# Feed-forward in-products by Strassen's scheme in a decoder trunk, with ScalarE copying products between PSUM banks

## The chip, the cores and the metric

One NeuronCore of a Trainium2 chip runs the whole program in one launch. The metric is the device time of that core in microseconds. All arithmetic is in 32-bit floats.

## The reference

One inference step of a two-layer decoder on 544 tokens: 512 of a prompt and 8 samples with 4 tokens each. Layer 0 mixes tokens with RWKV-7, layer 1 with sparse attention. Before and after each mixer stands a half-step feed-forward, so there are four of them, each with its own weights:

```python
def swiglu(x, w_in, w_out):
    gate, up = jnp.split(x @ w_in, 2, axis=-1)
    return (jax.nn.silu(gate) * up) @ w_out

h = h + 0.5 * swiglu(rms_norm(h, g[0]), ffn_w_in[l, 0], ffn_w_out[l, 0])
h = h + mixer(rms_norm(h, g[1]))
h = h + 0.5 * swiglu(rms_norm(h, g[2]), ffn_w_in[l, 1], ffn_w_out[l, 1])
```

The model width is 1024 (8 tiles of 128 features), the feed-forward width 2816 (22 tiles). So `x @ w_in` has 22 gate and 22 up tiles.

## The kernel before

Activations lie with features on the partitions and the 544 tokens along the row, in two halves of 272 (`HALF`), since a PSUM bank holds 512 floats. The residual is `hT`, 8 tiles of 544.

Every feed-forward product keeps its precision by splitting both operands in a high part in TensorE's reduced format (`fp32r`) and a low part (the rest). ScalarE copies a weight slot from `raw` to `wh` (the high part, L1133), VectorE subtracts it to get `wl` (L1484), and TensorE computes high x high + high x low + low x high. That is the helper `times` (L518): three matmuls for each weight tile and half. Each matmul has a weight load of its own.

The work of a feed-forward `f` is in stages that share two slots `s` (two buffers in `raw`, `wh` and `wl`, four PSUM banks each): `inA` with 12 of the 22 feature tiles, `outA`, `inB` with 10, `outB`. One slot of an in-stage is one feature tile: 8 input tiles for gate (banks 4s, 4s+1) and 8 for up (banks 4s+2, 4s+3), 96 matmuls. VectorE scales the gate by the reciprocal root `rr` (L1553), ScalarE takes silu (L1194), VectorE multiplies with the up part (L1556), ScalarE copies the high part to `hh` (L1196) and VectorE makes the low part `hl` (L1560). One slot of an out-stage is one of 8 output tiles: VectorE scales it (L1582) and adds it to `hT` (L1586). In the last out-stage ScalarE squares the new `hT` tile (L1177) and VectorE sums the squares in `acc` (L1522); from these come the norm's sum on TensorE (L509), the root on ScalarE (L1184) and the reciprocal on VectorE (L1526).

The operand of an in-stage is `xh` (ScalarE, L1163) and `xl` (VectorE, L1532), `hT` times the norm's gain; the root is applied afterwards through `rr`. In the second and fourth feed-forward the operand is made as the stage before (`wo` and `bo`) ends, and the norm comes in the first in-slot, between its gate and its up.

The order on each engine is the order in the program. `pipeline` on ScalarE and VectorE puts the split of the next slot before the finishing of this one. SP's queue brings the weights: `stream_split` waits for `w_split[s]`, then loads 1 MB for an in-slot. Semaphores named here: `landed[s]` (weights there), `w_hi[s]`, `w_split[s]`, `multiplied[s]` (TensorE is through), `taken[s]` (the banks are free), `gate_done`, `hid_hi`, `hid_done`. GpSimd issues other loads and has arithmetic only in the mixers (L2057, L2147).

## Time and profile before

| what | value |
|---|---|
| median of 3 runs | 2955.61 us (2951.46 to 2957.7) |
| the profiled execution: own time | 2960.64 us |
| its span | 2959.0 us |
| TensorE busy (matmul / weight load) | 2794.9 us (94%) / 2551.7 us (86%) |
| VectorE, ScalarE, GpSimd busy | 1185.8 us (40%), 806.5 us (27%), 282.6 us (10%) |
| matmuls | 25,177 |
| mean granted clock of TensorE | 0.942 |

The span is the time from the first instruction to the last one; the own time is what the same execution took as a whole. The busy share of matmuls is an upper bound, since they are pipelined. The granted clock is a share of 2.4 GHz; 0.5 is 1.2 GHz.

### The profile page before, as it was taken

How to read it: one execution, taken by the hardware profiler on the slowest of the kernel's cores; microseconds unless marked ns; L12 is line 12 of the kernel's file. 1: busy time of each engine (PE TensorE's matmuls, PEld its weight loads, DVE VectorE, ACT ScalarE, POOL GpSimd, SP SyncE). 2: the span in 40 equal slices, each digit the busy share in tenths (PEclk: the TensorE clock that was granted, in tenths of full speed). 3: DMA queues.
4: the chain of work that ended last, by engine and by line, in shares of the span. 5: the costliest groups of instructions: out<-in, count | busy, mean ns of one | idle time of the engine just before them, and what ended most of it. 6: DMA issues, size and time to landing. Idle time of an engine off the chain costs nothing. (4 is left out here: it accounts for less than half of the span.)

```text
span 2959.0 us, 56832 instructions
## 1 busy us (share of the span) xinstructions
PE 2794.9 (94%) x25177; PEld 2551.7 (86%) x25177; DVE 1185.8 (40%) x1738; ACT 806.5 (27%) x1261; POOL 282.6 (10%) x288
## 2 busy tenths in 40 slices
PE   7999969998999899999998989999998889999997
PEld 7999966776899746999997879999995568999997
DVE  4333355176333251433334123333444443433335
ACT  4212212132222100222221053212226762322221
POOL 1000000001111110000001200000007860000000
PEclk9999989999998557999998999999998997999998
DMA  6222210210000000322224622222222010222222
GB/s 233 82 89 86 77 64 15 71 58 30 4 3 4 33 29 26 131 82 80 95 69 120 162 100 85 85 100 85 71 74 65 23 44 29 88 90 79 99 69 75
DMA packets 36806, 214.84 MB, mean 73 GB/s; under 512 B 5232, under 2 KB 5360, under 8 KB 20880
## 3 DMA queue, kind: packets, MB, share of 16 engines
q1 hardware_dynamic: 27936, 174.34, 17.1%
q0 software_dynamic: 8720, 38.28, 4.4%
q8 instruction: 121, 1.98, 0.3%
q14 instruction: 29, 0.24, 0.0%
HBM read 202.49 MB, written 12.17 MB: 73 GB/s over the span
## 5 line engine op out<-in xcount | busy, mean ns | idle before, releaser
L518 PE MATMUL banks<-xh,wh 128*128 128x272 f32 x3072 | 638.7, 289 | 30.3 <-DVE wl L1484 18.0
L518 PE MATMUL banks<-xh,wl 128*128 128x272 f32 x3072 | 637.5, 289 | 0.0
L518 PE MATMUL banks<-xl,wh 128*128 128x272 f32 x3072 | 635.0, 288 | 0.0
L518 PEld LDWEIGHTS banks<-xh,wh 128*128 128x128 f32 x3072 | 485.5, 189 | 31.1 <-DVE wl L1484 23.4
L518 PEld LDWEIGHTS banks<-xl,wh 128*128 128x128 f32 x3072 | 484.7, 189 | 0.0
L518 PEld LDWEIGHTS banks<-xh,wl 128*128 128x128 f32 x3072 | 481.2, 189 | 0.0
L1484 DVE TENSOR_TENSOR wl<-raw,wh 128x2048 fp32r<-128x2048 f32 (+2 forms) x160 | 323.9, 2024 | 109.8 <-ACT wh L1133 109.7
L1133 ACT ACTIVATE wh<-raw 128x2048 fp32r<-128x2048 f32 (+2 forms) x160 | 270.7, 1692 | 260.5 <-PE banks L518 243.9
L518 PE MATMUL banks<-hh,wl 128*128 128x272 f32 x1408 | 291.4, 288 | 0.0
L518 PE MATMUL banks<-hh,wh 128*128 128x272 f32 x1408 | 291.0, 288 | 0.0
L518 PE MATMUL banks<-hl,wh 128*128 128x272 f32 x1408 | 290.2, 288 | 0.0
L1194 ACT ACTIVATE sg<-sg 128x544 f32<-128x544 f32 x88 | 58.1, 660 | 700.6 <-DVE sg L1553 700.6
L1553 DVE TENSOR_TENSOR sg<-banks,rr 128x544 f32<-128x544 f32 x88 | 63.8, 725 | 439.5 <-PE banks L518 439.5
L586 PE MATMUL banks<-arena,raw 128*128 128x272 f32 x896 | 209.9, 398 | 13.0 <-DVE arena L1540 10.4
L518 PEld LDWEIGHTS banks<-hh,wh 128*128 128x128 f32 x1408 | 221.4, 188 | 0.0
L518 PEld LDWEIGHTS banks<-hl,wh 128*128 128x128 f32 x1408 | 221.3, 189 | 0.0
L518 PEld LDWEIGHTS banks<-hh,wl 128*128 128x128 f32 x1408 | 219.8, 189 | 0.0
L586 PEld LDWEIGHTS banks<-arena,raw 128*128 128x128 f32 x896 | 172.6, 193 | 51.0 <-issue 14.9
L1582 DVE SCALAR_TENSOR_TENSOR sg<-banks,rr 128x544 f32<-128x544 f32 x64 | 46.4, 725 | 243.1 <-PE banks L518 243.1
L665 PE MATMUL banks<-arena,raw 128*128 128x272 f32 x512 | 120.4, 394 | 4.1 <-issue 4.1
L665 PEld LDWEIGHTS banks<-arena,raw 128*128 128x128 f32 x512 | 96.6, 190 | 27.3 <-issue 7.8
L2147 POOL TENSOR_SCALAR arena<-arena,stats 128x128 f32<-128x128 f32 (+3 forms) x108 | 116.0, 1087 | 40.6 <-DVE stats L1943 40.3
(301 smaller groups left out, 3030.6 us busy)
## 6 DMA issues: line engine op xcount, KB each, us to landing
raw<-in_w_in SPq DMA_DIRECT2D x88, 1024.0 KB, 4.8
raw<-in_w_out SPq DMA_DIRECT2D x32, 768.0 KB, 4.2
raw<-in_w_out SPq DMA_DIRECT2D x32, 640.0 KB, 3.9
raw<-in_w_rk SPq DMA_DIRECT2D x8, 1024.0 KB, 4.8
arena<-in_pages_c POOLq DMA_DIRECT2D x32, 256.0 KB, 7.6
raw<-in_w_kv SPq DMA_DIRECT2D x6, 1024.0 KB, 4.8
raw<-in_w_v SPq DMA_DIRECT2D x4, 1024.0 KB, 4.8
raw<-in_w_o SPq DMA_DIRECT2D x4, 1024.0 KB, 4.8
```

What stands on the lines that cost most here:

```text
L518: ins = mm(pst[:, bank + half, 0:HALF], wt[:, s, w], a[:, half * HALF:(half + 1) * HALF], start=first, stop=last)
L586: last = mm(pst[:, 4 * s + 2 * m + half, 0:HALF], w, src[:, ft, half * HALF:(half + 1) * HALF], start=(ft == 0), stop=(ft == DT - 1))
L665: last = mm(pst[:, 2 * w0 + half, 0:HALF], w, src[:, ft, half * HALF:(half + 1) * HALF], start=(ft == 0), stop=(ft == DT - 1))
L1133: act.activation(wh[:, s, 0:cols], raw[:, s, 0:cols], ACT.Copy).then_inc(w_hi[s], 1)
L1194: act.activation(sg[:, s, :], sg[:, s, :], ACT.Silu).then_inc(gate_done[s], 1)
L1484: dve.tensor_tensor(wl[:, s, 0:cols], raw[:, s, 0:cols], wh[:, s, 0:cols].bitcast(F32), ALU.subtract)\
L1553: dve.tensor_tensor(halves(sg[:, s, :]), bank2(4 * s), halves(rr[:]), ALU.mult)\
L1582: dve.scalar_tensor_tensor(out=halves(sg[:, s, :]), in0=bank2(4 * s), scalar=factor, in1=halves(rr[:]), op0=ALU.mult, op1=ALU.mult)\
L2147: ins = pool.tensor_scalar(s[:, c], s[:, c], stats[:, x, 4, 3 * p + n:3 * p + n + 1], None, ALU.mult)
```

## The change

The in-product of one feature tile, `[1024 inputs] x [gate and up] x [2 token halves]`, is taken as a 2 x 2 by 2 x 2 product of blocks: the inputs in even and odd tiles (4 each), the outputs in gate and up, the tokens in their two halves. Strassen's scheme in Winograd's form gives it by seven block products in place of eight, with sums of operand blocks ahead and sums of products behind. A block product is one token half with 4 weight tiles: 12 matmuls (`eighth`), so a slot has 84.

- Weights: of each slot VectorE makes four sums of 512 elements (`sums_w`), and the split to high and low goes by seven parts of 512 (`ring_h` on ScalarE, `ring_l` on VectorE), each as soon as TensorE has used the same part of the slot before.
- Operands: four sums in each of the four pairs of input tiles, by GpSimd (`operand_sums`); their high parts by ScalarE, their low parts by VectorE (`low_operands`). They are made once for each feed-forward, in its opening.
- Products: TensorE accumulates in bank x; ScalarE copies x to bank y, later x to w and x to z, and w to `sg`, and TensorE accumulates further products on these copies. VectorE adds the two results for up. All four banks are then the slot's gate and up. In the first two slots of a feed-forward 6 extra matmuls go to banks y and z.
- Stages: four in-stages (6, 6, 6 and 4 feature tiles) and four out-stages for each feed-forward. The first pair of slots of an out-stage is interleaved tile by tile. Out-stages A to C have 6 tiles a slot, D has 4.
- The reciprocal root (`inverse_root`) stands in VectorE's first in-slot between the second and third part; the root goes to `rr` and no longer to `sg`.
- Some of GpSimd's loads wait for the end of in-stage D (`part_split`).

The core of the diff. The block product:

```diff
+            def eighth(bank, quarter, f, b, js, start, stop):
+                for j in js:
+                    w = slice((4 * quarter + j) * P, (4 * quarter + j + 1) * P)
+                    xh_j, xl_j = xop_h[f][j][:, b, :], xop_l[f][j][:, b, :]
+                    for wt, x, first, last in ((ring_h, xh_j, start and j == 0, False), (ring_h, xl_j, False, False),
+                                               (ring_l, xh_j, False, stop and j == 3)):
+                        ins = mm(pst[:, bank, 0:HALF], wt[:, w], x, start=first, stop=last, skip_group_check=True)
+                return ins
```

TensorE, one in-slot (the first of a feed-forward has another order, as its operands come one by one):

```diff
+                pe.wait_ge(taken[s], i + k0)
+                part(0)
+                    eighth(x_bank, 0, f, 0, range(4), True, True).then_inc(eighth_done, 1)
+                    part(1)
+                    eighth(w_bank, 1, f, 5, range(4), True, True).then_inc(eighth_done, 1)
+                    part(2)
+                    snapped(1)
+                    eighth(x_bank, 2, f, 4, range(4), False, True).then_inc(eighth_done, 1)
+                    part(3)
+                    eighth(y_bank, 3, f, 1, range(4), False, True).then_inc(eighth_done, 1)
+                    part(4)
+                    snapped(3)
+                    eighth(x_bank, 4, f, 3, range(4), False, True).then_inc(eighth_done, 1)
+                pe.wait_ge(w_split[s], i + (ks + 1))
+                eighth(w_bank, 5, f, 6, range(4), False, True).then_inc(eighth_done, 1)
+                part(6)
+                snapped(4)
+                eighth(z_bank, 6, f, 2, range(4), False, True).then_inc(multiplied[s], 1)
```

ScalarE, slot `t`; `following(e)` is the high part `e` of slot `t + 1`:

```diff
+                    act.wait_ge(eighth_done, 6 * k + 1)
+                    act.activation(y, x, ACT.Copy).then_inc(snap, 1)
+                    following(0)
+                    act.wait_ge(eighth_done, 6 * k + 2)
+                    act.activation(sg[:, s, 0:HALF], w, ACT.Copy).then_inc(snap, 1)
+                    following(1)
+                    act.wait_ge(eighth_done, 6 * k + 3)
+                    act.activation(w, x, ACT.Copy).then_inc(snap, 1)
+                    if t == 0 and n is not None:
+                        norm(n, 4)
+                    if t:
+                        tail(t - 1)
+                    following(2)
+                    act.wait_ge(eighth_done, 6 * k + 4)
+                    following(3)
+                    act.wait_ge(eighth_done, 6 * k + 5)
+                    act.activation(z, x, ACT.Copy).then_inc(snap, 1)
+                    following(4)
+                    act.wait_ge(eighth_done, 6 * k + 6)
+                    following(5)
+                    act.wait_ge(multiplied[s], k0 + t // 2 + 1)
+                    following(6)
+                    act.wait_ge(taken[s], k0 + t // 2 + 1)
+                    act.activation(sg[:, s, :], sg[:, s, :], ACT.Silu).then_inc(gate_done[s], 1)
```

VectorE, slot `t`; `following(e)` is part `e` of slot `t + 1` (for `e` under 4 a weight sum first, then the low part):

```diff
+                    following(0)
+                    following(1)
+                    if t:
+                        tail(t - 1)
+                    if t == 0 and before:
+                        before()
+                    following(2)
+                    following(3)
+                    dve.wait_ge(snap, 4 * k + 4)
+                    dve.tensor_tensor(up[1], x, sg[:, s, 0:HALF], ALU.add).then_inc(up_done, 1)
+                    following(4)
+                    dve.wait_ge(eighth_done, 6 * k + 6)
+                    dve.tensor_tensor(up[0], w, sg[:, s, 0:HALF], ALU.add).then_inc(up_done, 1)
+                    following(5)
+                    dve.wait_ge(multiplied[s], k0 + t // 2 + 1)
+                    dve.wait_ge(up_done, 2 * k + 2)
+                    dve.tensor_tensor(halves(sg[:, s, :]), pst[:, 4 * s + 2:4 * s + 4, 0:HALF], halves(rr[:]), ALU.mult)                       .then_inc(taken[s], 1)
+                    following(6)
+                    dve.wait_ge(gate_done[s], h)
+                    dve.tensor_tensor(halves(sg[:, s, :]), halves(sg[:, s, :]), up_both, ALU.mult)                       .then_inc(hid_ready[s], 1)
```

TensorE, the first pair of slots of an out-stage:

```diff
+                for x in range(2):
+                    pe.wait_ge(hid_done[x], hidden + tiles // 2 - 1)
+                for s in range(2):
+                    take_split(s, k0, ks)
+                    for ft in range(tiles - 2):
+                        tile(s, ft)
+                pe.wait_ge(hid_done[0], hidden + tiles // 2)
+                for s in range(2):
+                    tile(s, tiles - 2)
+                pe.wait_ge(hid_done[1], hidden + tiles // 2)
+                for s in range(2):
+                    tile(s, tiles - 1).then_inc(multiplied[s], 1)
```

GpSimd, for each pair `j` of input tiles:

```diff
+                pool.wait_ge(xg_done, 8 * f + 2 * j + 1)
+                pool.tensor_tensor(t1, b12, b11, ALU.subtract).then_inc(t_step, 1)
+                pool.wait_ge(xg_done, 8 * f + 2 * j + 2)
+                pool.wait_ge(t_step, 8 * f + 2 * j + 1)
+                pool.tensor_tensor(t2, b22, t1, ALU.subtract).then_inc(t_step, 1)
+                pool.tensor_tensor(t3, b22, b12, ALU.subtract)
+                pool.wait_ge(t_step, 8 * f + 2 * j + 2)
+                pool.tensor_tensor(t4, b21, t2, ALU.subtract).then_inc(xt_done, 1)
```

## Rows read from the trace of the kernel before

**Rows 1.** The page: busy shares, and the granted clock in 40 slices.

```profile
PE 2794.9 (94%) x25177; PEld 2551.7 (86%) x25177; DVE 1185.8 (40%) x1738; ACT 806.5 (27%) x1261; POOL 282.6 (10%) x288
...
PEclk9999989999998557999998999999998997999998
```

**Rows 2.** Windows of the four feed-forwards: stretch, its length, busy us, clock, DMA.

```profile
18.00:432.00 414.00, 402.35 (x3176) 400.78 (x3176) 169.74 (x165) 104.00 (x103) 7.43 (x13) 0.99 0.30 100
...
sum 1620.00, PE 1602.11 PEld 1599.82 DVE 651.50 ACT 420.87 POOL 11.90; mean PE 400.53 PEld 399.96 DVE 162.87 ACT 105.22 POOL 2.98
```

**Rows 3.** Waits of TensorE: us in total, times, longest.

```profile
PE banks L518 <- DVE xl L1532: 7.1, 1, 7.1
```

**Rows 4.** Timeline of TensorE in an in-slot: start, us, instruction.

```profile
99.74 0.41 PE L518 MATMUL banks<-xh,wh 128*128 128x272 f32 x2
...
105.75 0.41 PE L518 MATMUL banks<-xh,wh 128*128 128x272 f32 x2
```

**Rows 5.** Timeline of VectorE: the scaling at a slot's end.

```profile
118.73 0.72 DVE L1553 TENSOR_TENSOR sg<-banks,rr 128x544 f32<-128x544 f32 x1 [4.93 <-PE banks L518]
```

**Rows 6.** Timeline of VectorE: operations back to back.

```profile
429.75 0.69 DVE L1635 TENSOR_TENSOR arena<-arena 128x511 f32<-128x511 f32 x1
430.36 0.15 DVE L1636 TENSOR_SCALAR arena<-arena 128x1 f32<-128x1 f32 x1
...
2492.71 5.17 DVE L2011 TENSOR_TENSOR xl<-arena,xh 128x544 fp32r<-128x544 f32 x8
```

**Rows 7.** Groups by line and shape on VectorE: count, busy us, mean ns.

```profile
L1484 DVE TENSOR_TENSOR wl<-raw,wh 128x2048 fp32r<-128x2048 f32 x96 | 220.0, 2292 | 94.9 <-ACT wh L1133 94.8
...
L1532 DVE SCALAR_TENSOR_TENSOR xl<-arena,const,xh 128x544 fp32r<-128x544 f32 x40 | 30.2, 781 | 15.9 <-ACT xh L1163 15.9
...
L1526 DVE RECIPROCAL rr<-sg 128x544 f32<-128x544 f32 x7 | 24.9, 3550 | 9.8 <-ACT sg L1184 9.8
...
L1926 DVE CUSTOM_DVE_ANT_0 arena<-banks,arena 128x256 f32<-128x256 f32 x26 | 10.2, 423 | 13.0 <-PE banks L988 13.0
```

**Rows 8.** Groups by line and shape on ScalarE.

```profile
L1133 ACT ACTIVATE wh<-raw 128x2048 fp32r<-128x2048 f32 x96 | 182.8, 1904 | 90.6 <-PE banks L518 74.0 <-PE banks L1096 10.3 <-DMA raw<-in_w_in 4.8
L1194 ACT ACTIVATE sg<-sg 128x544 f32<-128x544 f32 x88 | 58.1, 660 | 700.6 <-DVE sg L1553 700.6
...
L1423 ACT ACTIVATE arena<-banks 128x256 f32<-128x256 f32 x16 | 5.2, 379 | 14.7 <-PE banks L1004 14.7
```

**Rows 9.** Timeline of VectorE in the last out-stage of the first feed-forward.

```profile
374.30 0.72 DVE L1582 SCALAR_TENSOR_TENSOR sg<-banks,rr 128x544 f32<-128x544 f32 x1 [2.35 <-PE banks L518]
...
376.90 0.73 DVE L1522 TENSOR_TENSOR acc<-acc,sg 128x544 f32<-128x544 f32 x1 [0.99 <-ACT sg L1177]
...
381.81 0.72 DVE L1582 SCALAR_TENSOR_TENSOR sg<-banks,rr 128x544 f32<-128x544 f32 x1 [2.34 <-PE banks L518]
```

**Rows 10.** Timeline of VectorE in the first mixer: two operations of one size.

```profile
841.44 2.48 DVE L1723 TENSOR_TENSOR arena<-arena,const 128x1024 f32<-128x1024 f32 x1
843.95 1.22 DVE L1725 TENSOR_TENSOR arena<-arena,const 128x1024 f32<-128x1024 f32 x1
```

**Rows 11.** Timeline of GpSimd in the same stretch.

```profile
840.47 2.37 POOL L2057 TENSOR_TENSOR arena<-arena,const 128x1024 f32<-128x1024 f32 x1 [36.80 <-DVE arena L1718]
```

**Rows 12.** Timeline of VectorE at the openings: ends of slot 1, and of `wo`.

```profile
46.57 0.72 DVE L1553 TENSOR_TENSOR sg<-banks,rr 128x544 f32<-128x544 f32 x1 [4.96 <-PE banks L518]
...
1209.13 1.36 DVE L1588 SCALAR_TENSOR_TENSOR arena<-banks,arena 128x544 f32<-128x544 f32 x2 [5.50 <-PE banks L586]
...
1234.10 0.72 DVE L1553 TENSOR_TENSOR sg<-banks,rr 128x544 f32<-128x544 f32 x1 [4.93 <-PE banks L518]
...
1792.31 0.72 DVE L1553 TENSOR_TENSOR sg<-banks,rr 128x544 f32<-128x544 f32 x1 [4.93 <-PE banks L518]
```

**Rows 13.** The page: DMA issues, count, KB each, us to landing.

```profile
raw<-in_w_in SPq DMA_DIRECT2D x88, 1024.0 KB, 4.8
```

**Rows 14.** Timeline of GpSimd at the third feed-forward's opening.

```profile
1763.30 4.09 POOL L2118 DMA_DIRECT2D out_s_winv<-arena x8
```

511 lines of the change are left out of this document (371 added, 140 removed).

## Prediction

> **What bounds the kernel now.** I read the page's busy shares first: TensorE is busy 94% of the span, VectorE 40%, ScalarE 27% [rows 1]. Then the four feed-forward stretches together: in 1620 us TensorE is busy 1602 us at a granted clock of 0.99 in the first (2.4 GHz), VectorE 651, ScalarE 421 [rows 2]. Then TensorE's waits: in these stretches there are only the openings, such as 7.1 us at the third feed-forward [rows 3]. So matmuls set the pace there, and what they cost is their number times their spacing. In the timeline 48 matmuls of 272 columns take 105.75 - 99.74 = 6.01 us, 0.125 us each [rows 4]; an in-slot (96 of them) takes 12.02 us, and VectorE waits 4.93 us of it for the slot's end [rows 5].
>
> **What is removed.** Seven products of 12 matmuls stand in place of eight: 84 x 0.1252 = 10.52 us for a slot, 1.50 less. There are 88 slots (22 in each of four feed-forwards): -132 us. Each matmul already has a weight load of its own today, so that a weight tile now serves one column half changes nothing in their spacing. The matmuls of the out-stages stay the same.
>
> **The steady in-slot: can the others keep 10.5 us?** VectorE gets 4 sums and 7 splits of 512 elements where it had one split of 2048, 2 additions of 272 out of PSUM, and keeps 3 operations of 544. Back to back, a 511-element operation starts the next after 430.36 - 429.75 = 0.61 us, and eight of 544 take 5.17 us, so (5.17 - 0.72) / 7 = 0.64 each [rows 6]; 272 I place by the 256-element operation out of PSUM that takes 0.42 [rows 7], 0.37 back to back. 11 x 0.61 + 3 x 0.64 + 2 x 0.37 = 9.4 us. ScalarE: a copy takes 0.186 + 0.83 ns per element by its 2048 and 544 forms [rows 8], so 0.61 (0.54 back to back) for 512; seven of them, four copies between banks, silu and the hidden copy (0.57 each, 0.66 with its end) are 7 x 0.54 + 4 x 0.30 + 1.14 = 6.1 us. No row shows ScalarE writing PSUM; the 256-element copy out of PSUM takes 0.38 [rows 8], and the 2048 form's slope alone gives 0.23: I take 0.39 for 272, and 0.6 (what 512 cost) as the upper bound.
> Placed in the slot (0 = TensorE's start, a product every 1.50 us): the first bank copy runs 1.6 to 2.0 and is wanted at 3.0; the third 4.55 to 4.95, wanted at 6.0; the fourth 7.55 to 7.95, wanted at 9.0. VectorE starts its next slot's parts at 2.3, waits from 4.8 to 5.5 for the hidden copy (behind the third bank copy on ScalarE), then does ten operations and reaches the scaling of the finished slot at 10.6, which ends at 11.3; silu follows until 12.0 = 1.5 of the next slot, and then ScalarE is free for the first copy. So VectorE is back at 2.2 to 2.3 and TensorE doesn't wait: 10.5 us. The margin is 0.7 us of VectorE's idle time, and 0.6 us on the chain scaling, silu, first bank copy, third product. In-order ScalarE is what hands a late VectorE on to TensorE. Upper bound for this term: 0.05 us more for each of VectorE's 16 operations is absorbed, 0.1 more makes the slot 11.0, +44 us. It can't go below 10.52.
>
> **What is added where stages meet.** There are now four in- and four out-stages per feed-forward.
> (a) Start of in-stages B, C, D: VectorE comes from the last out-slots with 8 operations ahead and behind each other. It ends the first slot's splits at 5.1 instead of about 2.3, the second copy of the next slot's parts on ScalarE waits for its sum, and behind it stands the third bank copy: ready at 6.75, wanted at 6.0. 0.75 x 12 = 9 us (between 0 and 1.5 each).
> (b) First pair of out-slots: the tiles of both slots are interleaved, so both end at once (8.3 and 9.0 us), where today the second covers the first. Slot 2 needs VectorE's 1.5 us of addition [rows 9] and a split of 768 elements: by the 2048 form (2.29) and one of 544 (0.72) an element costs 1.04 ns [rows 5, 7], so 0.96. Ready at 10.7, TensorE waits 1.7. x 12 (A to C) = 20 us (15 to 25).
> (c) Out-stage D has 4 tiles: 24 matmuls = 3.0 us per slot. VectorE needs from 374.30 to 377.63 for scaling, addition, the wait for ScalarE's square and its sum [rows 9], 3.3 us, and 0.61 for the split: 3.9 us. Today that hides in a slot of 381.81 - 374.30 = 7.5 us. Laid out slot by slot from the first (ready at 5.3) the stage ends at 33.8 and not 27.0: 6.8 us, x 3; the third has the low parts of q's operand too (0.70 more per slot, their 0.78 [rows 7] less the overlap), 11 us. Sum 31 us (20 to 45).
> (d) Openings of stage A. The operands must be prepared in 16 pieces: GpSimd makes 4 sums for each of 4 pairs, at 2.37 us per 1024 elements [rows 11] some 0.76 us each, 3 us per pair; ScalarE 3.2 us per pair. The two opening slots have 6 extra matmuls each (1.5 us in all). The reciprocal (3.55 us [rows 7], at the norm) now stands between parts on VectorE, and silu and the first bank copy of the second slot wait behind it on ScalarE. For the second feed-forward (TensorE free at 1209.1): ScalarE ends its operand work at 1217.1, first bank copy 1217.5, slot 0 ends 1226.4; root at 1223.3, reciprocal to 1226.9, ten operations, scaling to 1232.1, silu, copy: the third product of slot 1 starts at 1233.2, the slot ends at 1240.7. Before it ended at 1234.1 [rows 12]: +6.6, and 3.0 because (removed) already counts both slots: 9.6 us. The fourth is alike, 9.6. The third: GpSimd first issues eight DMAs until 1767.4 [rows 14], last operand sum at 1779.8, slot 1 ends near 1802 where it ended at 1792.3 [rows 12]: 12.9, and 1 for a cold clock. The first: splits end at 30.3, squares are summed until 36.8, then norm, root and reciprocal to 42.9; slot 1 ends at 56.6 against 46.6 [rows 12]: 10 + 3 = 13. Together 46 us (30 to 65).
> (e) VectorE beside GpSimd. While GpSimd runs a two-input operation, VectorE's of the same size takes 2.48 us and not 1.22 [rows 10, 11]. GpSimd has this work only in the openings, 12 us in each, and most of it lies before the critical splits; I add 1 us for each, 4 in all (0 to 15). This is the rule of the Trainium skill, page "SBUF — State Buffer", section "Who interferes with whom": a VectorE instruction with two SBUF inputs contends with GpSimd's reads. By that rule, too, the sum is 4 us or, if all of the overlap is on the path, that of rival 5.
> Transfers are the same bytes; a slot's 1 MB lands in 4.8 us [rows 13], issued when VectorE has split part five of the slot two ahead, some 6 us before its first sum. Moved GpSimd loads (second LoRA weights, compression weights, attention tables) now start at the end of in-stage D, 30 us or more before their use: nothing.
>
> **Sum.** -132 + 9 + 20 + 31 + 46 + 4 = -22 us, against the profiled execution's own time of 2960.64 (span 2959.0): 2939. The median of the runs shown is 2955.6, 0.17% below that execution; so 2934. Nearly every uncertain term errs upwards, and I take 2936.
>
> **Rivals.**
> 1. VectorE paces the steady slot (other side). Point: 22 / 88 = 0.25 us, that is a slot of 10.8 us or more, and the gain is gone. Against: 9.4 us of work by rows that hardly vary (0.61, 0.64). For: 16 operations and twice as many semaphores cross three engines in each slot, and the margin is 0.6 us. At 11.0 us: 2936 + 44 = 2980. Chance 0.24.
> 2. The stage ends cost twice what I count (the clock falls when TensorE waits 1 us in 4 in D, or the straight-line code of VectorE and ScalarE is fetched late): +25 to +50, 2955 to 2985, about no change at the near end. For: between the first and second feed-forward, with short waits and small matmuls, slices show a granted clock of 0.5 [rows 1]; against: 0.99 in the first feed-forward in spite of its broken opening [rows 2]. Chance 0.20.
> 3. The stage ends overlap better (half of a to d): 53 us less, 2883. Chance 0.14.
> 4. The matmuls gain nothing, as one bank is now written by 12 in a row and not by two in turn: then +110 us, 3065. Against: each streams 272 columns, and no wait between them shows today. Chance 0.03.
> 5. The low operands of the openings (4 pairs of 2.3 us, 9 us) are all delayed by GpSimd by as much, and all of it is on the path: 37 us in place of 4, 2969. For: the doubled duration [rows 10]; against: TensorE waits there for ScalarE's queue first (d). Chance 0.03. It is the page named in (e) that speaks for it.
> The forecast's own case (2915 to 2950): 0.36.
>
> **How the numbers follow.** A measurement of this kernel can tell about 0.2% (6 us) from no change. Faster than 2949.7: the forecast's case, rival 3, and a little of rival 2: 0.58. Within 0.2%: most of the near end of rival 2 and a part of rival 1: 0.14. Slower: 0.28. Range: from most of rival 3 to rival 1's and 2's values: 2896 to 2985. The likeliest case's own range is 2915 to 2950.
>
> **What would show it.** Right: in-slots of 10.5 us on TensorE with VectorE about 90% busy; matmuls 0.125 us apart; the groups <- ScalarE and <- VectorE in TensorE's waits sum to some 100 us, 31 of it in the four D out-stages, where VectorE is never idle; 46 in the openings; scaling starts within 0.2 us of a slot's last matmul. Wrong: in-slots of 11 us or more with waits before the third product (rival 1), a granted clock of 0.5 within a feed-forward (rival 2), GpSimd's sums overlapping the splits on the path, or bank copies above 0.6 us.

## The result and the profile after

The changed kernel takes 2980.9 us (median of 14) where the kernel before takes 2956.6 (median of 14, in turns on the same chip): ratio 1.0087, 95% interval 1.0055 to 1.0118. The forecast was 2936, 0.7% faster, so its sign is wrong; that the time lies within the stated range of 2896 to 2985 is owed to its rivals 1 and 2. One of the 14 runs (3017.3 us), and one of the four of experiment 8 (3029.3 us), were in a slower state and count in the medians, but not in the ratios. The profiled execution took 2978.13 us (span 2976.5), 39 us more than the 2939 that the sum gave on that basis.

The page of the changed kernel, its busy shares and the granted clock in 40 slices; they answer to [rows 1]:

```profile
PE 2699.4 (91%) x24169; PEld 2442.5 (82%) x24169; DVE 1757.2 (59%) x2986; ACT 1157.7 (39%) x2228; POOL 353.2 (12%) x352
...
PEclk9999999999998657999999989999998997999998
```

TensorE's busy time fell by 95.5 us and not by 132 (126 with the 48 extra matmuls of the openings), while the span grew: TensorE waits more, and some of its matmuls run at half the clock, which counts as busy. Its waits (us in total, times, longest), which in the feed-forwards before were the 7.1 us of [rows 3], the start and the norms':

```profile
PE banks L580 <- DVE wl L1749: 49.5, 33, 3.8
PE banks L619 <- DVE ring_l L1806: 40.5, 5, 16.5
PE banks L619 <- DVE xop_l L1823: 19.6, 6, 7.0
...
PE banks L619 <- ACT banks L1419: 19.2, 5, 7.0
...
PE banks L619 <- ACT banks L1430: 8.1, 13, 0.7
```

L580 is the out-slots (waits for VectorE's split), L619 the in-slots; `ring_l` is the low part of an in-slot's weights, `xop_l` that of the operand sums, `wl` that of an out-slot's weights. L1419 is ScalarE's first copy between banks, L1430 its third. 16.5 us of the second line is the start, before any work. Without it these five lines are 120 us, where some 100 were forecast.

**The steady in-slot** is as forecast. The timeline of the changed kernel from one scaling (L1899) to the next:

```profile
90.17 0.73 DVE L1899 TENSOR_TENSOR sg<-banks,rr 128x544 f32<-128x544 f32 x1
...
91.67 0.38 ACT L1419 ACTIVATE banks<-banks 128x272 f32<-128x272 f32 x1
...
95.63 0.73 DVE L1868 TENSOR_TENSOR hl<-sg,hh 128x544 fp32r<-128x544 f32 x1 [0.77 <-ACT hh L1404]
...
100.64 0.72 DVE L1899 TENSOR_TENSOR sg<-banks,rr 128x544 f32<-128x544 f32 x1
```

10.47 us, where 10.52 was expected, and VectorE's only longer idle time in it is 0.77 us. So the gain of 132 us is there, and all of it and 18 us more is lost elsewhere: the stage ends and openings cost some 150 us, where 110 were forecast. To see where, I split each feed-forward at the scaling that ends its slot 1 and at its last out-slot's addition. "Opening" is the time to the first of them, from the last additions of `wo` or `bo` for the second and fourth (a row of two, as in [rows 12]), from the copy of 2176 elements for the third, from the start of the span for the first; "body" is the time between the two.

| us | opening 1, 2, 3, 4 | body 1, 2, 3, 4 | sum of the eight |
|---|---|---|---|
| before | 46.6, 25.0, 32.4, 25.0 | 372.8, 372.8, 372.8, 372.8 | 1620.2 |
| forecast | 56.6, 31.6, 43.3, 31.6 | 357, 357, 361, 357 | 1595 |
| changed | 69.2, 35.2, 51.2, 36.6 | 359.1, 358.7, 368.3, 361.0 | 1639.3 |

The forecast's row is from its terms: openings (d) without the 3 us that (removed) counts twice, bodies 372.8 - 20 x 1.50 + a quarter each of (a) and (b) + the stage's own part of (c). The changed kernel misses it by 29 us in the openings and 15 in the bodies, 44 in all; 4 of them are term (e), and the stretches between the feed-forwards add up to some 1.5 us less than before. That is the 39.

**The first opening.** The timeline of the changed kernel:

```profile
32.12 0.59 PE L619 MATMUL banks<-xop_h,ring_h 128*128 128x272 f32 x1 [11.31 <-DVE ring_l L1806]
...
34.45 1.19 ACT L1354 ACTIVATE sg<-arena 128x544 f32<-128x544 f32 x2
...
36.95 0.66 ACT L1354 ACTIVATE sg<-arena 128x544 f32<-128x544 f32 x1 [1.31 <-DVE acc L1835]
...
41.66 0.38 ACT L1419 ACTIVATE banks<-banks 128x272 f32<-128x272 f32 x1
...
42.18 0.57 PE L619 MATMUL banks<-xop_h,ring_h 128*128 128x272 f32 x1 [6.97 <-ACT banks L1419]
...
49.45 0.71 ACT L1384 ACTIVATE rr<-banks,eps 128x544 f32<-128x544 f32 x1
...
69.24 0.72 DVE L1899 TENSOR_TENSOR sg<-banks,rr 128x544 f32<-128x544 f32 x1
```

ScalarE has eight squares (L1354) to make, each waiting for VectorE's sum of the one before but one, and the copy that TensorE needs (L1419) stands behind the last of them: 7.0 us of waiting, and the norm, the root and the reciprocal follow late. Set beside the forecast, the splits end 6 us late (at 36.3 for 30.3; the operands wait for GpSimd's sums), the squares take the 6.5 us that were forecast, and from them to the end of the reciprocal it is 11 us in place of 6.

**The third opening**, in the timeline:

```profile
1765.37 1.26 POOL L2387 TENSOR_TENSOR arena<-arena 128x272 f32<-128x272 f32 x1
1765.94 1.25 DVE L1806 TENSOR_TENSOR ring_l<-arena,ring_h 128x512 fp32r<-128x512 f32 x1
...
1768.48 0.75 POOL L2393 TENSOR_TENSOR arena<-arena 128x272 f32<-128x272 f32 x1
...
1770.40 1.60 DVE L1823 TENSOR_TENSOR xop_l<-arena,xop_h 128x1088 fp32r<-128x1088 f32 x1 [3.22 <-ACT xop_h L1350]
...
1770.81 1.82 POOL L2391 TENSOR_TENSOR arena<-arena 128x272 f32<-128x272 f32 x1
...
1782.75 1.80 POOL L2393 TENSOR_TENSOR arena<-arena 128x272 f32<-128x272 f32 x1
1784.59 1.11 ACT L1350 ACTIVATE xop_h<-arena 128x1088 fp32r<-128x1088 f32 x1 [4.48 <-POOL arena L2393]
...
1787.16 0.38 ACT L1419 ACTIVATE banks<-banks 128x272 f32<-128x272 f32 x1
```

GpSimd's sum takes 0.75 us alone and up to 1.82 beside VectorE, and VectorE's operations beside it take 1.25 (alone 0.69) and 1.60 (alone 1.29). Counted from the copy of 2176 elements, at which this opening begins, the sixteen sums start after 7.5 us, as forecast, and end after 26.6, where 19.9 was forecast: 6.8 us late, of the 7.9 by which the whole opening is later than forecast. ScalarE's last operand (L1350) waits 4.48 us for GpSimd. And TensorE has the lower clock for part of these stretches. The windows of the four openings (stretch, its length, busy us and instructions of TensorE's matmuls, its weight loads, VectorE, ScalarE and GpSimd, then granted clock and DMA):

```profile
16.00:70.00 54.00, 32.19 (x192) 30.75 (x193) 41.36 (x55) 31.00 (x51) 18.00 (x20) 0.97 0.43 148
1212.00:1248.00 36.00, 27.58 (x193) 26.78 (x192) 28.42 (x40) 20.10 (x36) 4.24 (x4) 0.86 0.26 88
1758.00:1810.00 52.00, 29.41 (x189) 27.97 (x190) 39.75 (x50) 30.39 (x49) 24.46 (x26) 0.70 0.14 43
2562.00:2600.00 38.00, 27.71 (x184) 26.68 (x182) 29.06 (x41) 21.78 (x37) 4.21 (x4) 0.82 0.18 59
```

What the lower clock costs there can be estimated from the matmuls' starts. In the four openings, leaving aside the first matmul behind each wait, 154 start 0.19 to 0.3 us after the one before, where 0.125 is usual; before the change there were 38. At 0.1 us each that is 12 us more, 2 of them in the third opening; where another wait follows, it hides part of it.

**The bodies.** Here there is something that the forecast had as a rival only. The first pair of out-slots of the third feed-forward, in the timeline:

```profile
1861.77 0.51 PE L580 MATMUL banks<-hh,wh 128*128 128x272 f32 x2 [1.78 <-DVE wl L1749]
...
1862.83 0.65 PE L580 MATMUL banks<-hh,wh 128*128 128x272 f32 x2
1863.28 0.66 PE L580 MATMUL banks<-hl,wh 128*128 128x272 f32 x2
...
1866.65 0.41 PE L580 MATMUL banks<-hl,wh 128*128 128x272 f32 x2
1866.90 0.41 PE L580 MATMUL banks<-hh,wl 128*128 128x272 f32 x2
...
1868.09 0.72 DVE L1927 SCALAR_TENSOR_TENSOR sg<-banks,rr 128x544 f32<-128x544 f32 x1 [4.20 <-PE banks L580]
```

The wait of 1.78 us is the 1.7 of (b). But behind it two matmuls are 0.45 us apart (the lower of the clock's two levels) for 3 us, and only then 0.25. In such places additions are 6.6 us apart, in the others 5.0; it is so in 3 of the 12 pairs, though TensorE waits 1.78 us in all twelve. In the last out-stages it is so twice: in the fourth feed-forward (6.1 for 3.5, behind a wait of 2.96, while the same wait in the first and second has none behind it) and in the third (5.05 for 4.3). That is 7 to 8 us together. How many such stretches there are changes from execution to execution: over 13 runs of this kernel time and mean granted clock go together, from 2965.7 us at 0.939 to 3006.0 at 0.924, and the profiled one (2978.1, 0.933) is one draw.

The steady slots of the last out-stage are as forecast, 3.8 us by VectorE's work for 3.0 of matmuls:

```profile
409.60 0.72 DVE L1927 SCALAR_TENSOR_TENSOR sg<-banks,rr 128x544 f32<-128x544 f32 x1
...
413.44 0.72 DVE L1927 SCALAR_TENSOR_TENSOR sg<-banks,rr 128x544 f32<-128x544 f32 x1
```

Behind the last out-stage of the third feed-forward there is a wait and a slow stretch again, larger:

```profile
2175.27 2.29 DVE L1749 TENSOR_TENSOR wl<-raw,wh 128x2048 fp32r<-128x2048 f32 x1 [0.85 <-ACT wh L1287]
...
2177.62 0.82 PE L580 MATMUL banks<-xh,wh 128*128 128x272 f32 x2 [3.57 <-DVE wl L1749]
2178.24 0.66 PE L580 MATMUL banks<-xl,wh 128*128 128x272 f32 x2
2178.69 0.66 PE L580 MATMUL banks<-xh,wl 128*128 128x272 f32 x2
```

`q`'s first weights, 1.90 + 2.29 us of splitting for 2048 elements, were hidden beneath an out-slot of 7.5 us; an out-slot of 3.0 us hides little of it. TensorE waits 3.57 us and is slow until 2183.2.

### The profile page after: what moved, and what is told of

Its sections match the earlier page's. It is cut to its first block, busy times and chain, and to the rows that moved or that the text cites. A ratio compares the mean times of both kernels' runs of the same rounds, so it can differ in the third digit from the quotient of the medians.

```text
span 2976.5 us, 58599 instructions
## 1 busy us (share of the span) xinstructions
PE 2699.4 (91%) x24169; PEld 2442.5 (82%) x24169; DVE 1757.2 (59%) x2986; ACT 1157.7 (39%) x2228; POOL 353.2 (12%) x352
## 3 DMA queue, kind: packets, MB, share of 16 engines
q8 instruction: 140, 2.29, 0.3%
## 4 chain that ended last, share of the span: by engine, by line
PE 74%; DVE 11%; issue 6%; POOL 4%; ACT 3%; DMA 1%; POOLq 0%; DVEq 0%; ACTq 0%; SPq 0%
PE banks L619 28%; PE banks L580 17%; PE banks L740 7%; PE banks L819 4%; PE banks L875 3%; DVE ring_l L1806 2%; DVE sg L1927 1%; POOL arena L2525 1%; PE banks L1031 1%; DVE arena L1931 1%; DVE wl L1749 1%; PE banks L1058 1%; PE banks L771 1%; PE banks L1158 1%; PE banks L1216 1%
## 5 line engine op out<-in xcount | busy, mean ns | idle before, releaser
L619 PE MATMUL banks<-xop_h,ring_h 128*128 128x272 f32 x2480 | 725.7, 293 | 87.4 <-DVE ring_l L1806 40.5
L619 PE MATMUL banks<-xop_l,ring_h 128*128 128x272 f32 x2480 | 720.8, 291 | 0.0
L619 PE MATMUL banks<-xop_h,ring_l 128*128 128x272 f32 x2480 | 719.8, 290 | 0.0
L619 PEld LDWEIGHTS banks<-xop_h,ring_h 128*128 128x128 f32 x2480 | 474.9, 191 | 94.7 <-issue 31.2
L619 PEld LDWEIGHTS banks<-xop_h,ring_l 128*128 128x128 f32 x2480 | 474.6, 191 | 0.0
L619 PEld LDWEIGHTS banks<-xop_l,ring_h 128*128 128x128 f32 x2480 | 474.0, 191 | 0.2
L580 PE MATMUL banks<-hh,wh 128*128 128x272 f32 x1408 | 298.2, 293 | 46.1 <-DVE wl L1749 45.9
L580 PE MATMUL banks<-hh,wl 128*128 128x272 f32 x1408 | 294.6, 291 | 0.0
L580 PE MATMUL banks<-hl,wh 128*128 128x272 f32 x1408 | 294.0, 291 | 0.0
L1325 ACT ACTIVATE ring_h<-arena 128x512 fp32r<-128x512 f32 x352 | 220.8, 627 | 130.2 <-PE banks L619 59.9
L580 PEld LDWEIGHTS banks<-hh,wh 128*128 128x128 f32 x1408 | 224.3, 191 | 53.4 <-DVE arena L1931 23.9
L1806 DVE TENSOR_TENSOR ring_l<-arena,ring_h 128x512 fp32r<-128x512 f32 x352 | 242.7, 690 | 9.1 <-ACT ring_h L1325 7.8
L580 PEld LDWEIGHTS banks<-hl,wh 128*128 128x128 f32 x1408 | 224.7, 191 | 0.0
L580 PEld LDWEIGHTS banks<-hh,wl 128*128 128x128 f32 x1408 | 223.5, 192 | 0.0
L1325 ACT ACTIVATE ring_h<-raw 128x512 fp32r<-128x512 f32 x264 | 165.2, 626 | 88.0 <-PE banks L580 43.9
L1806 DVE TENSOR_TENSOR ring_l<-raw,ring_h 128x512 fp32r<-128x512 f32 x264 | 181.7, 688 | 0.3 <-ACT ring_h L1325 0.2
```

Of the source, the lines that this page charges most:

```text
L580: ins = mm(pst[:, bank + half, 0:HALF], wt[:, s, w], a[:, half * HALF:(half + 1) * HALF], start=first, stop=last)
L619: ins = mm(pst[:, bank, 0:HALF], wt[:, w], x, start=first, stop=last, skip_group_check=True)
L1325: act.activation(ring_part(ring_h, e), weight_part(s, e), ACT.Copy)\
L1806: ins = dve.tensor_tensor(ring_part(ring_l, e), weight_part(s, e), ring_part(ring_h, e).bitcast(F32), ALU.subtract)
```

## The experiments

All times below are beside runs of the kernel before on the same chip. A profile is one execution, and outside the feed-forwards it varies by up to 19 us (from the last out-slot of the first feed-forward to slot 1 of the second it is 808 to 827 us in the profiles of the changed kernel and of experiments 1 to 4), so single terms are read from the table of openings and bodies. Each edit is made on the changed kernel. "Theory A" and "theory B" are those of the expectation that stands above each result.

**1. Stages of 4, 6, 6, 6 tiles.** (e1_sizes)

```
-FT_IN = (6, 6, 6, 4)
+FT_IN = (4, 6, 6, 6)
```

> The four stages of a feed-forward take 4, 6, 6, 6 hidden tiles in place of 6, 6, 6, 4, so that the stage whose out-slots carry the squares and, in the third, q's operand has out-slots of 4.5 us on TensorE and not 3.0. Theory A (VectorE's 3.8 us of work per slot of the last out-stage, 4.3 in the third, sets its pace, and q's first 2048-element split stands uncovered in a 3.0 us slot): the waits before these out-slots go, 0.8 x 7 = 6 us for each feed-forward, 9 in the third, and half of q's 3.6 us wait with the half clock behind it; the first out-stage gets slots of 3.0 us in which VectorE has 2.1 us of work, and loses 1 to 2 us at its end. Together 20 to 25 us less than the changed kernel, 2955 against 2978, and no wait above 1 us before the last out-stage's slots 3 to 8. Theory B (a stage of 4 tiles costs the same wherever it stands, since its tiles are too few for the turn-round from in- to out-slots): less than 5 us.

2978.8 us, ratio 1.0065 (1.0034 to 1.0097): nothing gained. Bodies 360.3, 359.9, 361.9, 359.9. Theory B in the sum. The steady out-slots of the last stage did go to 4.5 us, but the first pair there got worse: its additions stand 3.8 and 6.5 us apart in the first feed-forward (2.3 and 5.0 in stages without a slow stretch, here as in the changed kernel), since VectorE has two slots of 3.8 us on its hands at once: TensorE waits 3.3 us for the third slot's split, and has the lower clock for part of what follows (4.5 us of matmuls end 6.3 us after their start). All four first pairs of the last stage have such a slow stretch here, and 4 of the 8 of the middle stages. So theory A's waits did go, but others came: the third feed-forward gained 6.4 us and the fourth 1.1, the first two lost 1.2 each.

**2. The first two out-slots one after the other.** (e2_pair_order)

```
+                take_split(0, k0, ks)
+                for ft in range(tiles - 2):
+                    tile(0, ft)
+                take_split(1, k0, ks)
...
+                for ft in range(ahead):
+                    tile(1, ft)
+                pe.wait_ge(hid_done[0], hidden + tiles // 2)
+                tile(0, tiles - 2)
+                pe.wait_ge(hid_done[1], hidden + tiles // 2)
+                tile(0, tiles - 1).then_inc(multiplied[0], 1)
+                for ft in range(ahead, tiles - 1):
+                    tile(1, ft)
+                tile(1, tiles - 1).then_inc(multiplied[1], 1)
```

`ahead` is 1 of 6 tiles and 2 of 4. The lines take the place of those that took both slots tile by tile.

> The first two out-slots of each out-stage aren't interleaved to their ends: the second slot's first tiles only fill the time until the last hidden tiles are there, the first slot ends 3 us earlier (at about 5.3 of 9 us), and VectorE prepares the third under the second. Theory A (both slots end at once, VectorE's addition and split of the third slot stand uncovered, 1.8 us of TensorE's time, and behind some of these waits the clock falls to half for 3 us more): 12 pairs x 1.8 = 21 us and 4 half-clock stretches of 1.5 to 2.7 us less: 20 to 28 us, 2953 against 2978, no out-slot gap of 6.6 us, and fewer of 5.0. Theory B (TensorE waits for the last hidden tile of the stage instead, so that the gap only moves): under 6 us.

2950.4 us, ratio 0.998 (0.9947 to 1.0014), 30 us less than the changed kernel. Bodies 352.4, 353.3, 358.6, 351.8: 31 us less. The additions in the timeline of this kernel, same place as above:

```profile
1836.07 0.72 DVE L1932 SCALAR_TENSOR_TENSOR sg<-banks,rr 128x544 f32<-128x544 f32 x1 [1.35 <-PE banks L580]
...
1839.82 0.72 DVE L1932 SCALAR_TENSOR_TENSOR sg<-banks,rr 128x544 f32<-128x544 f32 x1 [1.40 <-PE banks L580]
...
1844.32 0.72 DVE L1932 SCALAR_TENSOR_TENSOR sg<-banks,rr 128x544 f32<-128x544 f32 x1 [2.15 <-PE banks L580]
```

3.75, 4.5, and 4.5 from there on: no wait, no slow stretch, and so in all twelve pairs. It is the same work in another order. Theory A. Of the 31 us, 25 are the twelve pairs (2.06 each), some 5 the slow stretches behind three of them, and 2 the first pairs of the last stages. Slow stretches are not gone from the kernel: three of its four last stages still have one, behind waits of 2.2 to 3.1 us.

**3. The squares behind the first bank copy, in the first opening.** (e3_squares)

```
             for e in range(1, 7):
                 weights("inA0", 0, e)
-            for ft in range(DT):
-                square(0, ft, ft % 2)
...
                     act.activation(y, x, ACT.Copy).then_inc(snap, 1)
+                    if k == 0:
+                        for ft in range(DT):
+                            square(0, ft, ft % 2)
```

> In the first feed-forward alone ScalarE's eight squares stand behind its first copy between banks, not ahead of it. Theory A (the first bank copy waits in ScalarE's queue behind squares that VectorE's sums pace, 7.0 us of TensorE's time): TensorE's second wait shrinks from 7.0 to about 1 us, the root comes from 49.5 to 45 us and slot 1 of the first feed-forward ends at 64.5 to 65.5 and not 69.2: 4 to 5 us less, 2974. Theory B (the norm's chain of squares, sums, root and reciprocal is what ends last in this opening, so that TensorE's wait only moves in front of the second slot): slot 1 ends at 68.5 to 69.2, no change.

The first opening is 63.8 us, 5.5 less. The timeline of this kernel:

```profile
35.12 0.38 ACT L1419 ACTIVATE banks<-banks 128x272 f32<-128x272 f32 x1 [0.76 <-PE banks L619]
...
35.41 1.20 ACT L1354 ACTIVATE sg<-arena 128x544 f32<-128x544 f32 x2
...
45.49 0.71 ACT L1384 ACTIVATE rr<-banks,eps 128x544 f32<-128x544 f32 x1
```

TensorE waits 0.62 us for the copy in place of 6.97, and the root comes 4.0 us earlier. Theory A. Part of the 5.5 is clock: 20 fewer matmuls of this opening have the slow spacing, 2 us. The whole is 2980.4 us, ratio 1.007 (1.0031 to 1.0108): 5 us in 2980 don't show in the medians; the opening's rows are what measured them.

**4. Operand sums by VectorE.** (e4_dve_sums)

```
+            def operand_sums(f, j):
...
+                dve.tensor_tensor(t1, b12, b11, ALU.subtract).then_inc(t_step, 1)
...
+                operand_sums(0, j)
                 low_operands(0, j, 0)
...
-            for j in range(4):
-                operand_sums(0, j)
```

The lines taken away are GpSimd's calls. It is so for all four sums (the third ahead of the second) and all four openings.

> The operand sums of the four openings (16 of 272 elements in each) are made by VectorE and not by GpSimd. Theory A (GpSimd is the slow one in the openings: its sums take 0.76 us alone and 1.2 to 1.8 beside VectorE, whose splits of 512 then take 1.25 in place of 0.69 and whose low operands take 1.6 in place of 1.05 and 1.29): VectorE gets 4 x 0.37 = 1.5 us more per pair but nothing of its work is stretched; openings shorten by 2 to 4 us in the first, 1 to 2 in the second and fourth, 8 to 12 in the third, where GpSimd starts behind eight DMA issues; slot 1 of the third ends near 1799 on the changed kernel's time line and not 1809. Together 12 to 20 us less, 2962. Theory B (VectorE is the fuller engine of the openings, and 6 us more for it in each cost as much as GpSimd's stretching): no change or up to 10 us more.

2971.0 us, ratio 1.0038 (1.0015 to 1.0062), 10 us less. Openings 66.9, 33.7, 44.9, 34.7: by 2.3, 1.5, 6.3 and 1.9 us, 12 in all, at the low end of what was expected. Theory A. The bodies of this profile are 5 us longer, with more slow stretches (5 of the 12 pairs).

**5. Short operand sums on GpSimd.** (e5_short_sums)

```
-                b11, b21, b22, t1, t2, t3, t4, b12 = (x[:, n, :] for n in range(8))
+                b11, b21, b22, t1, t2, t3, t4, b12 = (x[:, n, 0:8] for n in range(8))
```

> Work left out: GpSimd makes each of the operand sums of the four openings over 8 of 272 columns only (the rest of these operands is not summed). Waits and order stay as in the changed kernel; GpSimd clears the first three staging areas of the first feed-forward. Theory A (GpSimd's duration and its collision with VectorE are what the openings lose beside what I forecast): VectorE's low operands and splits come back to 1.05, 1.29 and 0.69 us, slot 1 of the openings ends 3 us earlier in the first, 2 in the second and fourth, 10 in the third (51.2 us after the copy of 2176 elements, now 41). That is more than moving the sums to VectorE gave (2.3, 1.5, 6.3, 1.9), by VectorE's 6 us of added work where it is on the path. Theory B (ScalarE's queue and the norm's chain set the ends): as with the sums on VectorE, or less.

2963.0 us, ratio 1.003 (1.0002 to 1.0058). Openings 63.1, 33.8, 44.7, 34.4: by 6.1, 1.4, 6.5 and 2.2, 16 in all. In the timeline GpSimd's sum takes 0.20 us and VectorE's low operand 1.29:

```profile
1762.60 0.20 POOL L2387 TENSOR_TENSOR arena<-arena 128x8 f32<-128x8 f32 x1
...
1763.82 1.29 DVE L1823 TENSOR_TENSOR xop_l<-arena,xop_h 128x1088 fp32r<-128x1088 f32 x1 [1.56 <-ACT xop_h L1350]
```

So GpSimd's own duration and its collision with VectorE cost 16 us together (this run does not part them); in three of the openings VectorE does the sums at nearly no cost, in the first its own added work takes most of it back. Theory A, with 6.1 in the first opening for the 3 expected, and 6.5 in the third for 10. The sums over the other 264 columns are left out here, so the kernel's result is not the reference's.

**6 and 7. One and two more operations of VectorE in each in-slot.** (e6_one_more, e7_two_more)

```
                     following(2)
+                    one_more(s)
                     following(3)
+                    one_more(s)
+                    dve.wait_ge(extra, len(extras))
```

`one_more` subtracts 512 elements of `rr` from themselves; the second call is in experiment 7 only.

> Every in-slot gets one more subtraction of 512 elements on VectorE (0.61 us back to back), whose result nothing uses, after its second split. Theory A (VectorE has 0.7 us to spare in a 10.5 us slot): the slots stay within 0.1 us, at most 9 us more for 88 slots, and scaling still starts within 0.2 us of a slot's last matmul. Theory B (the slot is already paced by VectorE's chain): 0.6 x 88 = 54 us more than the changed kernel, 3032.

> Every in-slot gets two more such subtractions of 512 elements on VectorE, 1.22 us. Theory A (0.7 us to spare): 0.5 us over in each slot, in-slots of 11.0 us, 88 x 0.5 = 44 us more than the changed kernel, 3022, with waits of TensorE before its third product. Theory B (the spare time is larger, since ScalarE's bank copies and silu hand a late VectorE on only in part): under 15 us more.

One more: 2984.2 us, ratio 1.0108 (1.0061 to 1.0154), 3 us more than the changed kernel, in-slots 10.5. Theory A. Two more: 3024.0 us, ratio 1.0225 (1.0172 to 1.0277), 43 more, in-slots 10.81. The timeline of the latter:

```profile
94.57 0.72 DVE L1913 TENSOR_TENSOR sg<-banks,rr 128x544 f32<-128x544 f32 x1
...
102.75 0.69 DVE L1818 TENSOR_TENSOR arena<-rr 128x512 f32<-128x512 f32 x1
...
105.38 0.72 DVE L1913 TENSOR_TENSOR sg<-banks,rr 128x544 f32<-128x544 f32 x1
```

Between these, VectorE has no idle time of note, so 10.81 us is the work of 18 operations, and 16 take 10.81 - 1.22 = 9.6. The spare time of the changed kernel's slot is 10.5 - 9.6 = 0.9 us (forecast: 9.4 of work and 0.7 of idle time). In the table the bodies are 28 us longer (367.1, 368.1, 373.4, 366.8) and the openings 10, where the added work delays slot 1. Theory A, with a slot of 10.8 for the 11.0 expected.

**8. One weight sum by GpSimd.** (e8_gp_sum)

```
-                if e == 2:
-                    if n:
-                        dve.wait_ge(part_split, 6 * n - 1)
-                    dve.tensor_tensor(s1, raw_part(s, 1, 0), raw_part(s, 1, 1), ALU.add).then_inc(dve_sums, 1)
...
+                        if n:
+                            pool.wait_ge(part_split, 6 * n - 1)
+                        pool.tensor_tensor(s1, raw_part(s, 1, 0), raw_part(s, 1, 1), ALU.add).then_inc(gp_sums, 1)
```

> One of the four weight sums of each in-slot (the one for part four) is made by GpSimd, and not by VectorE. Theory A (GpSimd and VectorE stretch each other where both read two SBUF operands: 0.76 us for 272 elements alone makes 1.4 for 512, 2.4 to 3 beside VectorE, and four of VectorE's operations in it take 1.25 in place of 0.69): VectorE saves 0.61 us per slot and loses 1.2 to 2.2, its spare time of 0.7 us goes, in-slots of 10.5 to 11.2 us, 0 to 60 us more. Theory B (GpSimd's reads fit in between, as VectorE has spare time): in-slots stay at 10.5 and VectorE's own work falls by 0.6 us, no change in time.

3001.6 us in the median of four; the three that count are 2979.8, 2990.1 and 3013.1, ratio 1.0188 (1.0116 to 1.0261). The changed kernel's own runs go from 2965.7 to 3006.0, so three runs tell little. The profile is of the first of these: in-slots stay at 10.5, the table's sum is 14 us above the changed kernel's, 9 of it in the openings. The collision is there:

```profile
82.59 1.29 POOL L2407 TENSOR_TENSOR arena<-raw 128x512 f32<-128x512 f32 x1 [9.19 <-DVE ring_l L1808]
82.89 1.53 DVE L1808 TENSOR_TENSOR ring_l<-raw,ring_h 128x512 fp32r<-128x512 f32 x1
```

VectorE saves 0.61 us and pays 1.53 - 0.69 = 0.84 in one operation. Giving the sum away doesn't relieve VectorE. In-slots that stay at 10.5 fit theory B and the low end of A; VectorE's work doesn't fall as B has it, and it loses less than A's 1.2 to 2.2 us, so neither holds whole. Why two of the runs were 10 and 33 us above the profiled one stays open.

**9. ScalarE's first copies ahead.** (e10_front)

```
+            def first_copy(f, t):
+                act.wait_ge(eighth_done, 6 * (IN_SLOTS[f"inA{f}"] + t) + 1)
+                act.activation(pst[:, 4 * t + 2, 0:HALF], pst[:, 4 * t, 0:HALF], ACT.Copy).then_inc(snap, 1)
...
+                    if t > 1 or not name.startswith("inA"):
...
+                    if t == 0 and name.startswith("inA"):
+                        first_copy(f, 1)
                     act.wait_ge(taken[s], k0 + t // 2 + 1)
                     act.activation(sg[:, s, :], sg[:, s, :], ACT.Silu).then_inc(gate_done[s], 1)
```

(and `first_copy(f, 0)` ahead of the high parts 4 to 6; the condition `t > 1` keeps slots 0 and 1 from copying a second time.)

> In the four openings ScalarE's first copy between banks of slot 0 stands ahead of its high parts 4 to 6 (in the first feed-forward ahead of the squares too), and the first copy of slot 1 ahead of silu of slot 0. Nothing else moves. Theory A (ScalarE's order of work hands the late chain to TensorE: 1.6 us of high parts before the first copy, 2.2 us in slot 1 behind silu, which waits for scaling, which waits for the reciprocal and ten operations of VectorE): slot 1 of the first feed-forward ends 7 us earlier, of the others 3 to 4 us, about 18 us in all, 2963 against 2981. Theory B (the root's chain sets the end of slot 1, so that these copies only move TensorE's waits): 5 us in the first feed-forward, as with the squares alone, and under 1 us in the others.

2966.9 us, ratio 1.0021 (0.9992 to 1.0049), 14 us less. Openings 65.5, 32.5, 51.2, 33.8: by 3.8, 2.7, 0 and 2.8, and the bodies of the last three are 1 to 3 us shorter, in part since their third slot comes 9.7 and not 10.5 us after the second; 15 us in the sum of the eight. Theory A in the second and fourth; the first gained less than the squares alone did (5.5). In the third slot 0 ends 1.4 us earlier, but silu now stands behind slot 1's first copy, VectorE waits 3.27 us for it (1.28 in the changed kernel), and slot 1's scaling comes no earlier; 0.8 us of the gain appears only with the third slot.

**10. Sizes and order together.** (e11_sizes_order)

> Both the stages of 4, 6, 6, 6 tiles and the first two out-slots one after the other. Sizes alone gave nothing: the last out-stage's steady slots went to 4.5 us, but its first pair, with both slots ending at once and 3.8 us of VectorE's work behind each, cost 3.8 + 6.5 us in place of 2.3 + 5.0. Theory A (that pair is what ate the gain of the sizes): with the pair in order the sizes give 3 to 5 us for each feed-forward on top of the order alone, 12 to 20 us, and this runs at about 2935, where the order alone ran at 2950. Theory B (VectorE's 3.8 us against 4.5 leaves too little, or the first stage with 4 tiles loses as much as the last did): 2950, bodies of 352 to 353 us from slot 1 to the last out-slot as with the order alone.

2925.2 us, ratio 0.9868 (0.983 to 0.9905). Bodies 348.1, 348.8, 352.1, 349.0: 18 us less than the order alone, 49 less than the changed kernel. Sizes alone gave 5 in the same sum of bodies. So the pair at the beginning of the last out-stage ate most of their gain. Theory A. This profile has no slow stretch in any body; some 4 of the 18 us are the three that the order alone still had.

**11 and 12. The versions that follow.** (e12_three: order, sums by VectorE, first copies ahead; e13_four: sizes as well)

> Three of the single edits together, with the stages of 6, 6, 6, 4 tiles: first two out-slots in order (31 us by the traces), operand sums of the openings by VectorE (12 us), ScalarE's first copies ahead (10 to 18 us). Theory A (they act on different stretches and add up): 2981 - 31 - 12 - 15 = 2923, 1.1% less than the kernel before the change. Theory B (the last two both shorten the openings, where one chain, the norm's, is left): 2935.

> As the kernel with three edits, with stages of 4, 6, 6, 6 tiles as well. If the sizes give their 3 to 5 us per feed-forward once the pair is in order: 2908. If not, as the kernel with three edits.

2920.8 us, ratio 0.9854 (0.9809 to 0.9898), and 2911.5 us, ratio 0.9825 (0.9787 to 0.9863). The edits add up. The last one is 1.75% faster than the kernel before the change, and 69 us faster than the change as it was made. Its table: openings 62.0, 29.1, 46.3, 30.4, bodies 347.2, 348.1, 351.2, 347.9, 77 us less than the changed kernel in the sum. The page and TensorE's longest waits:

```profile
PE 2685.3 (93%) x24169; PEld 2431.4 (84%) x24169; DVE 1764.5 (61%) x3050; ACT 1156.8 (40%) x2228; POOL 282.4 (10%) x288
```

```profile
PE banks L619 <- DVE ring_l L1824: 31.1, 3, 17.4
PE banks L776 <- DVE arena L2027: 19.5, 1, 19.5
PE banks L619 <- ACT banks L1443: 15.1, 19, 1.8
...
PE banks L580 <- DVE wl L1767: 8.3, 11, 2.5
```

The waits for VectorE's out-slot splits fell from 49.5 to 8.3 us. This version was expected at 2908, the one before it at 2923.

## Why the prediction was wrong

- **Removed, -132: right.** In-slots of 10.5 us, matmuls 0.125 apart; rival 4 fell.
- **The steady slot: right**; rival 1 fell. VectorE's work is 9.6 us (9.4 forecast), ScalarE's copies between banks 0.38 (0.39). The two forms of [rows 8] give a constant of 0.21 us for a copy, not the 0.186 of the working; that is 0.02 us each and changes nothing. Two further operations are needed to make VectorE the bound.
- **(a) Start of in-stages:** 15.0 us would be an out-slot and an in-slot, and the last out-slot's addition and the first scaling stand 6.2 + 9.9 = 16.1 after the one before: 1.1, and the next slot gives 0.2 of it back. So 0.9 for the 0.75 forecast: right in mechanism (TensorE waits up to 0.7 us for the third bank copy, L1430, 13 times) and some 2 us small over the twelve.
- **(b) First pair: right in mechanism, too small in price.** The wait is 1.78 us as worked out (1.7), twelve times; the half clock behind three of them, 1.5 us each, wasn't counted. It costs 27 us for 20. Experiment 2 gave back 31, more than this: its pairs end 0.2 us earlier than slots of 4.5 us would, and the last stages' first pairs gained too.
- **(c) Last out-stage: right in mechanism, too small.** Slots of 3.8 us, 4.3 in the third, as forecast. From its last scaling to its last addition the stage takes 31.1 us in the first and second feed-forward where eight slots of 3.0 would be 24: 7.1 for 6.8. In the fourth it is 9.6, with a slow stretch, and in the third 14.8 for 11. What I didn't cost at all is what comes next in the third: `q`'s first weights, 4.2 us of splitting behind a slot of 3.0. They had been hidden beneath a slot of 7.5; the shorter slot took that cover away, and I put the term at nothing without naming the work that would hide it. 2.6 us of it are in the body, and some 2.6 of half clock behind it.
- **(d) Openings: the step that failed.** They are 63 us later in all where 34 were expected, 29 of the 44 us that the forecast's row of the table misses. Two causes are shown. First, the step "ScalarE ends its operand work, first bank copy, slot 0". In the first feed-forward I placed the squares in VectorE's and ScalarE's time, and overlooked that the copy stands behind them in ScalarE's queue (5.5 us, experiment 3). In the second and fourth, the parts 4 to 6 ahead of the copy, and the first copy of slot 1 behind silu, cost some 3 us each (experiment 9). Second, GpSimd's sums, which I had at 3 us per pair, with 1 us per opening for the collision: 6.1, 1.4, 6.5 and 2.2 us in the four openings (experiment 5). Experiment 11, which has both repairs, takes 19.5 of the 29 us back. VectorE makes the sums there, and by experiments 4 and 5 keeps 4 us of the rest for it; some 6 us have no cause shown.
- **(e) VectorE beside GpSimd, 4 us: too small.** Without the sums' duration it is 16 us less (experiment 5), which holds GpSimd's time as well as the collision; the forecast allowed 1 us for each opening, and 3 us of GpSimd's time per pair, where the third needed 4.8. Both engines are stretched, and I had counted VectorE alone. The rule of the Trainium skill, page "SBUF — State Buffer", section "Who interferes with whom", had this collision, and the trace agrees that there is one: 1.25 us for 0.69. Rival 5, which priced it at 37 us, had the low operands doubled; they take 1.6 to 1.85 us beside GpSimd for 1.29 alone, so its mechanism was not what happened, and 16 is nearer to my 4.
- **The rival that came closest is 2**, and by its price more than by its words: 2955 to 2985 for 2978. It says that the stage ends cost twice what I count, which would be 106 us more; it is priced at 25 to 50, and the measured costs are 39 more, 1.4 times. Of its two reasons the clock was there in part: half-clock stretches in 3 of 12 pairs, in two last stages and behind `q`, and some 12 us in the openings by the estimate above. The other, code that is fetched late, doesn't show: among the waits that the profile lists for VectorE and ScalarE in the four feed-forwards, none is put down to `issue` (time in which an engine waits for nothing that the profile shows). I gave the rival 0.20, although I had written that nearly every uncertain term errs upwards.

The size of the whole was decided by the terms that no row of before showed as such, 110 us of costs against a firm 132, and each of them was laid out as a schedule by hand in which a missed queue entry can only add time. A sum of such terms wants a margin in one direction.

What stays open: how much of the openings' loss is the half clock and how much the waits that it follows, since no run parts them; how GpSimd's 16 us divide between its own time and the collision; some 6 us of the openings; and the spread of experiment 8.

## What to carry to other kernels

When a change trades TensorE's work for many small stages, the steady slot is the easy part; write out, for every stage boundary, each engine's queue in order and ask what stands ahead of the one small operation that TensorE waits for. Here moving a copy ahead, and letting one slot end before its neighbour, gave back some 44 us without a single operation less. When two slots that share an engine behind them end together, that engine's work for both comes into the open; let one end early. And a fix can be hidden by another: the stage sizes were worth next to nothing (2 us in the medians, 5 in the bodies) until the pair was in order, then 18 us in the bodies.

## What the runs showed of the hardware

- A wait of TensorE of only 1.8 us can be followed by 3 us at the lower clock, and waits of the same length elsewhere aren't: 3 of 12 alike places in the profile of the changed kernel. Between its runs, time and mean granted clock move together (2965.7 us at 0.939, 3006.0 at 0.924).
- GpSimd and VectorE slow each other down, not one the other: 272 elements take 0.75 us alone and up to 1.82 on GpSimd, 512 elements 0.69 alone and 1.25 (1.53 in experiment 8) on VectorE.
- ScalarE's copy of 272 elements from one PSUM bank to another takes 0.382 us, from PSUM to SBUF 0.397.
